# Delta rule rounds 5 to 8 on 32x32 diagonal blocks, in sets of 16 small matmuls

## What is computed

```python
def step(S, inp):
    qi, ki, vi, gi, bi = inp
    diff = gi[..., :, None] - gi[..., None, :]
    decay = jnp.exp(jnp.where(tril, diff, -jnp.inf))
    kb = ki * bi[..., None]
    lmat = jnp.where(strict, jnp.einsum('bhid,bhjd->bhij', kb, ki) * decay, 0.0)
    rhs = jnp.concatenate([vi * bi[..., None], kb * jnp.exp(gi)[..., None]], axis=-1)
    sol = lax.linalg.triangular_solve(lmat + eye, rhs, left_side=True, lower=True, unit_diagonal=True)
    ...
```

## Time and profile before

| | us |
|---|---|
| median of 3 runs | 2066.0 |
| lowest and highest | 2065.07, 2070.97 |
| the profiled execution, device time | 2072.88 |
| its span, first to last instruction | 2071.2 |

### The profile page before, as it was taken

One profiled execution on the slowest core, in us unless ns is written; L12 is line 12 of the kernel. 1 busy time (PEld: TensorE's weight loads), 2 busy tenths in 40 slices (PEclk: granted clock), 3 DMA queues, 4 the chain that ended last, 5 costly groups with the idle time before them and its releaser, 6 DMA issues.

```text
span 2071.2 us, 38366 instructions
## 1 busy us (share of the span) xinstructions
PE 1906.9 (92%) x14814; PEld 1776.6 (86%) x14814; DVE 1021.3 (49%) x1627; ACT 659.1 (32%) x1101; POOL 887.6 (43%) x753
## 2 busy tenths in 40 slices
PE   6999978787888999999998899888888999999998
PEld 4999968777886999999998899655557999999997
DVE  3787634565445453352456523455564353253352
ACT  3553322334331432221223122244443332222221
POOL 3444532343054654464558233000014854465465
PEclk9999989999998999999999999999999999999999
DMA  4122310000054523222222231477873422222221
GB/s 124 53 70 71 81 37 21 1 0 0 0 133 137 143 82 88 85 81 82 82 61 80 82 115 66 157 283 272 305 264 90 129 86 87 82 81 81 82 67 54
DMA packets 250357, 201.69 MB, mean 97 GB/s; under 512 B 7541, under 2 KB 230007, under 8 KB 250017
## 3 DMA queue, kind: packets, MB, share of 16 engines
q1 hardware_dynamic: 241092, 170.48, 27.5%
q10 hardware_dynamic: 9164, 29.80, 3.9%
HBM read 187.72 MB, written 12.53 MB: 97 GB/s over the span
## 4 chain that ended last, share of the span: by engine, by line
PE 76%; DVE 9%; ACT 4%; issue 4%; POOL 3%; DMA 2%; ACTq 1%; SPq 0%; DVEq 0%; POOLq 0%
PE PS L665 72%; DVE f L1311 4%; PE PS L668 4%; ACT f L1867 2%; DVE f L1414 1%; ACT f L1870 1%; POOL r L2318 1%; DVE f L1308 1%; POOL f L2308 1%; DMA f<-in_cache_k 1%; ACTq L2217 1%; DMA f<-in_a_w_in 1%; DVE r L1331 1%; ACT L1867 1%; ACTq L2215 0%
## 5 line engine op out<-in xcount | busy, mean ns | idle before, releaser
L665 PE MATMUL PS<-r,r 128*128 128x288 f32 (+2 forms) x9888 | 1322.8, 295 | 17.9 <-DVE r L1311 4.8
L665 PEld LDWEIGHTS PS<-r,r 128*128 128x128 f32 x9888 | 1305.8, 189 | 23.2 <-DVE r L1311 5.7
L1311 DVE TENSOR_TENSOR f<-PS,f 128x512 f32<-128x512 f32 (+10 forms) x463 | 227.5, 517 | 548.1 <-PE PS L665 522.2
L2463 POOL TENSOR_TENSOR r<-f,r 128x1024 fp32r<-128x1024 f32 x128 | 312.8, 2446 | 299.1 <-ACT r L1870 298.6
L1870 ACT ACTIVATE r<-f 128x1024 fp32r<-128x1024 f32 (+5 forms) x263 | 259.6, 998 | 489.7 <-PE PS L665 388.8
L665 PE MATMUL PS<-f,f 128*32 128x256 f32 (+14 forms) x2124 | 238.8, 375 | 40.6 <-POOL f L2308 12.9
L1870 ACT ACTIVATE f<-PS 128x512 f32<-128x512 f32 (+3 forms) x230 | 124.8, 561 | 374.4 <-PE PS L668 193.0
L2308 POOL TENSOR_TENSOR f<-f,f 128x512 f32<-128x512 f32 (+1 forms) x155 | 143.9, 948 | 228.6 <-DVE f L1311 150.5
L668 PE MATMUL PS<-f,f 128*128 128x128 f32 (+5 forms) x1226 | 176.5, 287 | 64.1 <-DVE f L1311 25.9
L665 PEld LDWEIGHTS PS<-f,f 128*32 128x32 f32 (+4 forms) x2124 | 145.5, 145 | 101.5 <-issue 63.4
L665 PE MATMUL PS<-f 128*128 128x128 f32 x1504 | 198.9, 293 | 34.1 <-ACT f L1870 23.5
(11 more groups left out here) (74 smaller groups left out, 708.2 us busy)
## 6 DMA issues: line engine op xcount, KB each, us to landing
f<-in_f_w_up SPq DMA_DIRECT2D x88, 512.0 KB, 3.9
f<-in_cache_k SPq DMA_DIRECT2D x64, 512.0 KB, 5.5
f<-in_cache_v ACTq DMA_DIRECT2D x56, 512.0 KB, 6.1
f<-in_a_w_in SPq DMA_DIRECT2D x32, 512.0 KB, 4.2
f<-in_f_w_down SPq DMA_DIRECT2D x32, 512.0 KB, 3.7
f<-in_a_w_out SPq DMA_DIRECT2D x16, 512.0 KB, 4.0
f<-in_w_kv SPq DMA_DIRECT2D x8, 1024.0 KB, 5.5
out<-f SPq DMA_DIRECT2D x13, 512.0 KB, 5.0
```

The lines of the kernel that those rows point to most:

```text
L665: return nc.tensor.matmul(out, lhsT, rhs, start=start, stop=stop)
L1311: return V.tensor_tensor(out, a, b, op)
L2463: G_.tensor_tensor(upW.lo2[n], upW.raw2[n], upW.hi_f[n], ALU.subtract).then_inc(w_lo, 1)
```

## The change

In rounds 5 to 8 only the 32x32 blocks on the diagonal of each head's 128x128 matrix are multiplied; E is zero outside smaller blocks than these. For a product of four heads and four blocks each, `spread` issues 16 matmuls of 32x32x32. Block m's operands lie on partitions 32m to 32m+31, and head n's result is written to partitions 32n to 32n+31 of bank m, so that each of the 16 has its own row and column tile of the array. The results of a round lie packed: 96 columns a bank, for E^T, E and P^T (`X_ET`, `X_E`, `X_PT`), and one copy takes them to a slot (`PK`); head and block change places in each round. P^T is no longer added on VectorE: `spread` runs twice into the same columns, once with the identity as the stationary operand and once with E, and PSUM adds the two; in round 5 the moving operand is the identity as well, so VectorE's addition in round 4 goes. Round 5 is evacuated by VectorE (384 columns), round 6 by ScalarE (384), round 7 by VectorE (256), round 8 by both, two copies of 32 partitions each, into the diagonal blocks of PT, which VectorE zeroes once ahead of the stage. Small matmuls in a round: 64, 64, 48, 32. TensorE's loop over chunks 1 to 3 is written out; the other engines keep theirs.

```diff
-DELTA_LINKS, DELTA_ACT, DELTA_POOL = 20, 7, 9
+DELTA_LINKS, DELTA_ACT, DELTA_POOL = 18, 5, 9
...
-        R_DVE = [1, 3, 4, 5, 6, 7, 8, 9, 10, 11, 12, 14, 16]
-        R_ACT = [1, 2, 4, 5, 6, 7, 9, 10, 11, 13, 15]
+        R_DVE = [1, 3, 4, 5, 7, 8, 9, 10, 11, 12, 14, 16]
+        R_ACT = [1, 2, 4, 6, 8, 9, 10, 11, 13, 15]
...
+        X_ET, X_E, X_PT = (slice(32 * n, 32 * n + 32) for n in range(3))
+
+        def part(n):
+            return slice(32 * n, 32 * n + 32)
+
+        def pack(G):
+            return G[:, PK, 0:4 * 96].rearrange("p (b n) -> p b n", b=4)
...
-                    elif r == 5:
-                        for u in range(4):
-                            mm(bk(2, u), sl(ET, u), sl(EE, u))
-                        for u in range(4):
-                            last = mm(bk(3, u), sl(EE, u), sl(ET, u))
-                    elif r == 6:
-                        for u in range(4):
-                            mm(bk(0, u), sl(E2, u), sl(PT, u))
-                        for u in range(4):
-                            mm(bk(1, u), sl(E2T, u), sl(E2, u))
-                        for u in range(4):
-                            last = mm(bk(2, u), sl(E2, u), sl(E2T, u))
-                    elif r == 7:
-                        for u in range(4):
-                            mm(bk(0, u), sl(E4, u), sl(PT, u))
-                        for u in range(4):
-                            last = mm(bk(1, u), sl(E4T, u), sl(E4, u))
-                    elif r == 8:
-                        for u in range(4):
-                            last = mm(bk(0, u), sl(E8, u), sl(PT, u))
+                    elif r in (5, 6, 7, 8):
+
+                        K = pack(G)
+                        last = None
+
+                        def spread(col, stationary, moving, first=True, final=True):
+                            for m in range(4):
+                                for n in range(4):
+                                    if r == 5:
+                                        c = slice(n * P + 32 * m, n * P + 32 * m + 32)
+                                        x = {"E": G[part(m), EE, c], "ET": G[part(m), ET, c]}
+                                    else:
+                                        x = {"E": K[part(m), n, X_E], "ET": K[part(m), n, X_ET],
+                                             "PT": K[part(m), n, X_PT]}
+                                    x["I"] = ident[part(m), part(m)]
+                                    ins = mm(PS[part(n), b[m], col], x[stationary], x[moving], first, final)
+                            return ins
+
+                        pt = "I" if r == 5 else "PT"
+                        if r < 8:
+                            spread(X_E, "ET", "E")
+                        if r < 7:
+                            spread(X_ET, "E", "ET")
+                        spread(X_PT, "I", pt, True, False)
+                        last = spread(X_PT, "E", pt, False, True)
...
-            with pe.Fori(1, NT) as i:
-                delta((0, 1), i, False, i + (-1))
+            for i in range(1, NT):
+                delta((0, 1), i, False, i - 1)
...
+                    banks = PS[:, 4 * g:4 * g + 4, :]
...
                     elif r == 4:
-                        link(copy(G[:, ET, :], b[1]))
-                        ins = tt(G4(PT), u4(b[1]), bu(ident, 4), ALU.add)
+                        ins = copy(G[:, ET, :], b[1])
                     elif r == 5:
-                        ins = copy(G[:, E2, :], b[2])
-                    elif r in (6, 7, 8):
-                        dve.wait_ge(gdv[g], len(R_DVE) * it + upto(R_DVE, r - 1))
-                        ins = tt(G[:, PT, :], b[0], G[:, PT, :], ALU.add)
+                        ins = copy(pack(G), banks[:, :, 0:96])
+                    elif r == 7:
+                        ins = copy(pack(G)[:, :, 32:96], banks[:, :, 32:96])
+                    elif r == 8:
+                        for n in range(2):
+                            ins = copy(u4(G[part(n), PT, :])[:, :, part(n)], banks[part(n), :, X_PT])
...
             dve.wait_ge(z_act, 8)
+            V.memset(gA[:, PT, :], 0.0)
+            V.memset(gB[:, PT, :], 0.0)
...
-                    elif r == 5:
-                        ins = copy(G[:, E2T, :], b[3])
                     elif r == 6:
-                        link(copy(G[:, E4, :], b[1]))
-                        ins = copy(G[:, E4T, :], b[2])
-                    elif r == 7:
-                        ins = copy(G[:, E8, :], b[1])
+                        ins = copy(pack(G), banks[:, :, 0:96])
+                    elif r == 8:
+                        for n in range(2, 4):
+                            ins = copy(u4(G[part(n), PT, :])[:, :, part(n)], banks[part(n), :, X_PT])
```

More of the change, by code:

```diff
@@ L431, in yoco_step @@
         (QS, KS, VS, DD, DA, DE, DR, KD, KHT, EE, RR, ATT, ET, PT, E2, E2T) = range(16)
-        KH, AM_, E4, E4T, E8, NN, NTT, DI, YY, N2, N2T, N4, TT, ZZ, TQ, VN, OO = (
-            KS, E2T, DD, DA, DE, DR, EE, ET, E2, E2T, DD, DA, DE, RR, ET, DR, EE)
+        KH, AM_, PK, NN, NTT, DI, YY, N2, N2T, N4, TT, ZZ, TQ, VN, OO = (
+            KS, E2T, E2, DR, EE, ET, E2, E2T, DD, DA, DE, RR, ET, DR, EE)
         GX = E2T
```

## The result

The changed kernel takes 2078.4 us (median of 11 runs) beside 2067.9 for the kernel before, measured on the same chip (11 runs): a ratio of 1.0046, 95% interval 1.0032 to 1.0059. It is slower by 0.5%, some 10 us, where 13 us less had been forecast. The profiled execution took 2079.7 us.

The account below looks back on a forecast made before the run. TensorE was taken as the bound in rounds 5 to 8, then ScalarE's block. Chunks 1 to 3 -6, chunk 0 -2, sample -5, loop -1, clock +1 make -13: 2066.0 becomes 2053 us; range 2028 to 2076.

Parts of the forecast that it names:

- The premise of ScalarE's block: Chunks 1 to 3: round 10 of group A hangs on ScalarE's table loads and scaling; starting them earlier gives -2.0 us each.
- the price of a packet: Rounds 5 to 8: 256 instructions of TensorE's code take 2.8 us to come, between 0.93 and 3.7.
- 4.4 packets and 1.5: Chunks 1 to 3, round 5 to round 8 of group A: 12.3 us for code packets plus 1.5 at the ends.
- second rival: Prompt chunks: a code packet costs 3.2 to 4 us there too; +3 us in all, 2069; chance 0.15.
- One such stretch more in each chunk: TensorE idling more may bring another stretch at 1.2 GHz per chunk: +7 us if so, 0 if none, taken as +1.
- Chunk 0: First prompt chunk, without ScalarE's block: +0.3 us with the same packets, -2.3 for code arriving meanwhile, so -2.0.
- Code arrives meanwhile: First prompt chunk: code comes in the 5 us between round 5 of group A and round 4 of B; -2.3 us.
- Sample: Sample chunk, packets at 3.7 us: ScalarE's block starts at 597 instead of 602.77, the wait for GpSimd goes; -5 us.
- Issue: Rounds 5 to 8: TensorE starts small-matmul records 7 ns apart, with 27 as the upper end; 2.9 us instead of 7.2.
- third rival: Rounds 5 to 8: TensorE issues only every 27 ns, 11.3 us a group instead of 7.2; +16, 2082; chance 0.18.
- The loop: Chunks 1 to 3 written out on TensorE save branch and register waits: 0 to -2 us, taken as -1.
- First rival: Delta stage: code arrives in time, so only issue and evacuation count; -38 us, 2028; chance 0.17.

Follow-up runs that it names:

- e10: The kernel before with only ScalarE's block moved from behind round 7 to behind round 3 of group B in prompt chunks; 2060.6 us, 0.9960.
- e5: The changed kernel with 64x64 blocks, E+I kept beside E, separate PSUM banks for E and E^T, and TensorE's loop kept; 2040.5 us, 0.9878.
- e9: e5 with ScalarE's block moved from behind round 7 to behind round 3 of group B in prompt chunks; 2030.5 us, 0.9813.
- e2: The changed kernel with E+I kept beside E, 144 small matmuls a group instead of 208, loop written out; 2051.5 us, 0.9917.
- e4: The changed kernel with the 16 identity matmuls of rounds 5 and 6 issued twice; 2090.5 us, 1.0113.
- e3: The kernel before with TensorE's loop over chunks 1 to 3 written out, nothing else; 2069.8 us, 1.0013.
- e6: e5 with TensorE's chunks 1 to 3 written out instead of the loop; 2039.9 us, 0.9871.
- e7: The changed kernel's instructions reordered so that one 32x32 tile's products follow each other; 2083.5 us, 1.0094.
- run 256: Not a follow-up run: in this sentence the words mean that TensorE executes 256 instructions, one packet of code.

## Why the prediction was wrong

**The premise of ScalarE's block: in part right before, gone after.** In the kernel before A10 waited 3.90 us for ScalarE, and in e10 1.42 for VectorE; e5 and e9 show the same once the code fits. But a block out of the way brought A10 forward by 1.5 us at most, so "what A5 to A8 save comes off the chunk" was too simple; most of what e9 and e10 gained is the clock behind the wait. The forecast said that A8 would end early enough to start the block 2 us earlier, and that B7, A9 and B8 would be done before it ends. In the trace it starts 0 to 1.8 us earlier, and A9, which stands behind B7's code, ends only after it: A10 now hangs on A9.

**The step that failed: the price of a packet.** "I take 2.8, nearer the upper end ...; it is under it because weight loads held the DMA engines then, and a prompt chunk has none." In the prompt chunks, with next to nothing else on the DMA engines, restarts come 3.45 to 4.00 us apart while a packet's transfer takes 1.06. So 3.7 us, as in the earlier trace rows, needs no contention. What a packet costs is mostly not transfer, and the reason given for going under the only measured interval was not one. At 3.7 the prediction's sum (4.4 packets and 1.5) gives 17.8 us from A5's start to A8's end, 467.1 and not the 466.5 that its second rival states; measured are 17.6 us to the start of A8's last matmul (449.11 to 466.73). That rival (2069, chance 0.15) has the mechanism, and e2 and e4 show it by removing and adding code. Its terms for the four prompt chunks add up to +8.5, and +9.0 was measured; what it lacks is the sample chunk, -5 against -1.0. The Trainium skill's Runtime: NRT & Kernel Launch (Instruction fetch mechanics), by which crossing into a new block of 256 instructions is mostly hidden, holds in e3 and e6 and not here: the four stops of 1.9 to 2.45 us are such crossings.

**The clock: the range was right, the choice was not.** "One such stretch more in each chunk would be +7, none 0: +1." Each prompt chunk got one: 13.6 to 20.5 us at 0.50 in rounds 5 to 9, as in the row of 454.80 to 475.20. A9's 20 records took 3.42, 3.66, 4.21 and 3.94 us from first to last start in the four chunks, against 2.11 for each of them before: 6.8 us, on the path, since A10 waits for A9. The output matmuls of the sample chunk lost 1.5 more (3.92 against 2.37). That is read from rows. No run changed the clock alone, and since the second rival's +8.5 has no clock in it, the 6.8 can't simply be added to it: how much of the loss is stops and how much clock stays open.

**Chunk 0 and the sample chunk.** Chunk 0: -2.0 forecast, +4.4 measured, by the same two terms. "Code arrives meanwhile" was not so: the 5 us from A5 to B4, in which it was to arrive, shrank to 2.4 (308.51 to 310.87), and all four stops were left. Sample: the price there was 3.7 in the forecast, so that is not its miss. Round 5 began 15.4 us after round 1 instead of 14.0, the block moved by 4.1 of the 5.8 us forecast, the wait for GpSimd went, and the stop in round 7 and the lower clock took back most of what that gave.

**What was right.** Issue: 7 ns taken, 8.6 measured. So the third rival's premise, 27 ns, is out for tiles that change. The Trainium skill's TensorE: Matmul & The Clock Gate (Wait — 56ns, not 53.3ns?) has a floor of about 25 ns; the trace does not agree, with 8.6 ns over 16 tiles and, in e7, 20 ns with a tile's products in a row. Slower was the outcome all the same, for the second rival's reason. 256 instructions to a packet, with stops put down to issue: right. A5's copy no earlier because of B3's operations on VectorE: right, B4 starts 19.4 us into the chunk instead of 19.7. The loop: -1 forecast; e3 has +2.7 (-0.4 to +5.6), so no gain, and little either way. First rival (code in time, 2028): e9 comes to 2030 and e5 to 2041 with code in time, but with other blocks and evacuations, so they do not test it.

**The stage as measured:** four chunks at +0.4 to +4.4 are +9.0, the sample chunk -1.0, together +8.0 for the stage, against -13.

## What to carry to other kernels

Count instructions beside columns: a matmul in fp32 is four here, and a stretch of this kernel that would run 256 of them in much under 3.5 us (1.3 us in the bursts) waited for its code. Before splitting matmuls as far as the array allows, try the next larger tile (64x64 here: 80 small matmuls a group instead of e2's 144, no stops in the chunk shown, 1.9% below the kernel before with one more line moved) and remove matmuls whose work an evacuation can do. When only one row shows a price, take that price; going under it needs a row too. And when a wait on TensorE's path is priced, look at the granted clock behind it as well.

## What the hardware showed that was not expected

- A loop of some 1,790 instructions on TensorE fetched its code again in its second pass (nine packets, 2.33 us of stop at its head), one of 1,270 fetched none. Where between them the limit lies was not tried.
- 32x32 matmuls start 8.6 ns apart over 16 tiles in turn and 20 ns apart with the products of one tile in a row, from the same instructions.
- The granted clock did not go with TensorE's busy time: 0.50 (1.2 GHz) in e7 with 19.95 of 20.30 us busy, mostly in 32x32 matmuls, and 1.00 (2.4 GHz) in rounds 5 to 9 of e5 with 9.74 of 15.90, by this row:

```profile
431.20:447.10 15.90, 9.74 (x349) 8.71 (x348) 10.35 (x20) 9.11 (x20) 2.40 (x4) 1.00 0.00 0
```
